# Two columns of x turned by VectorE from 32x32 blocks, and squares summed by ScalarE, in the front of a transformer block

## The chip, the cores and the metric

The kernel runs on one core of a Trainium2 chip. Its time is the device time of one execution in microseconds (us); the figure for a kernel is the median over its runs.

## What is computed

One layer of an encoder block in float32, with 1024 tokens and 1024 features. The part that the change touches is the first normalisation and the start of the combined projection:

```python
def rmsnorm(x, g):
    xf = x.astype(jnp.float32)
    y = xf * lax.rsqrt(jnp.mean(xf * xf, axis=-1, keepdims=True) + EPS)
    return (y * g.astype(jnp.float32)).astype(x.dtype)

h = rmsnorm(x, g_pre_mix[l])
proj = jnp.einsum('bsd,de->bse', h, w_in[l]) + b_in[l]
aq, ak, av, bq, bk, bv = jnp.split(proj, splits, axis=-1)
out_a = mixer_a(...)   # sliding window, 8 query heads on 2 key heads
out_b = mixer_b(...)   # chunked attention, 8 heads
y = jnp.einsum('bse,ed->bsd', mix, w_out[l])
x = x + rmsnorm(y, g_post_mix[l])
h = rmsnorm(x, g_pre_mlp[l])
u = jnp.square(jax.nn.relu(jnp.einsum('bsd,df->bsf', h, w_up[l])))
y = jnp.einsum('bsf,fd->bsd', u, w_down[l])
x = x + rmsnorm(y, g_post_mlp[l])
```

## The kernel before, in words

All engines run lists of instructions that are written out by hand and wait for each other by semaphores. SP's queue issues nearly all DMAs, in the order of its list; a wait in that list holds back every DMA behind it. TensorE (PE) multiplies, VectorE (DVE) and ScalarE (ACT) prepare its operands and take its results.

Every product is made of three, to keep float32 precision: an operand is split into a high part, rounded to the format `F32R`, and a low part, the difference. ScalarE makes the high parts (`x_hi`, `w1_hi`, `wv_hi`), VectorE the low ones (`x_lo`, `w1_lo`, `wv_lo`). The helper `three` issues the three matmuls; its lines in the trace are L2163, L2164 and L2165.

The front of the kernel goes by columns of x. A column k is 128 features of all 1024 tokens, 512 KB. It is loaded into `xraw[:, k]` with tokens on partitions, as eight tiles of 128 tokens. The matmul wants features on partitions, so TensorE turns each tile with a transpose (`x_transposes`, L2175, eight instructions for a column) into two PSUM banks. ScalarE copies the banks times the gain g to `x_hi` (L1064), VectorE forms `x_lo` (L1493), and TensorE then makes `first_products(k)`: three tiles of 128 outputs, two halves of 512 tokens, three matmuls each, 18 in all. TensorE's list per round is: transposes of column k + 1, products of column k. In the last round the transposes are those of `rcols` instead (L2235), a copy of 1/rms of each token spread over 128 columns, whose turning gives the row `rrow` by which the products are scaled later. After that come the value projections of two token tiles (48 matmuls of 320 columns each), which need `wv_hi` and `wv_lo` of all eight columns, and then attention.

The norm itself: ScalarE squares column k in one instruction of 1024 elements to one of two buffers (`square`, L1041), VectorE adds it to `sumsq` (`add_squares`, L1478). With all eight added, VectorE reduces over the 128 lanes of a tile (L1501) to `ss1`, one number for each token, ScalarE takes the root (L1069), VectorE forms 1/rms in five small steps (`rstd`, from L628) and writes the eight tiles of `rcols` (L1507). The tables `SQUARES` and `ADDED` say with which column each engine does what.

SP's queue loads the eight columns of x and the first weights in turn, then the tables, five of the value weights (`load_values`, 320 KB each), nine small constants and a bias row. It then waits until the last column is turned and squared, since the last three value weights are loaded over `xraw`. Behind them stand the stores and replication of the attention bias (`bias_rows`, `bias_a_rep`), the weights of a later tile (`load_fill(0)`, L698) and the biases of the first scores (`bias_a`, L681).

An exchange of 32x32 blocks followed by VectorE's transpose, which turns each 32x32 block by itself, is used further on in the kernel already: for attention probabilities (64 KB a DMA) and for the rows of the second norm (`hs`, 128 KB a DMA, L833, turned at L1790). There the data goes through a DRAM scratch and comes back in pieces of 32 floats.

## Time and profile before

| | before |
|---|---|
| median of three runs (lowest, highest) | 1037.47 us (1037.4, 1037.55) |
| the profiled execution: its time, its span | 1037.82 us, 1036.0 us |
| TensorE matmuls busy | 1026.4 us, 99% of the span |
| TensorE weight loads busy | 854.0 us, 82% |
| VectorE busy | 771.1 us, 74% |
| ScalarE busy | 467.8 us, 45% |
| GpSimd busy | 214.9 us, 21% |
| granted TensorE clock, mean | 0.998 of full |
| moved by DMA | 147.92 MB, 143 GB/s in the mean |

The span runs from the first to the last instruction that the profiler recorded; the time of the execution holds 1.8 us more. Busy time of TensorE overlaps itself, as matmuls are pipelined, so the distance from one start to the next is the cost of a matmul in a full list, not its length.

### The profile page before, as it was taken

The numbers are of one execution on the slowest core, as the hardware profiler recorded it, in microseconds if no ns is written. First come the engines' busy times: TensorE is split into PE (matmuls) and PEld (weight loads), VectorE is DVE, ScalarE is ACT, GpSimd is POOL, SyncE is SP. The second block draws the span as 40 slices with busy tenths as digits, with TensorE's granted clock in tenths as the row PEclk, the third lists the DMA queues.
The fourth block names the chain that finished last, engine by engine and source line by source line (L and its number), as shares of the span: only waits on it lengthen the run. The fifth ranks groups of instructions, "written<-read, shape, count | busy, mean of one in ns | idle before, by whom it ended". The sixth has DMA issues, their size and how long they took to land.

```text
span 1036.0 us, 15823 instructions
## 1 busy us (share of the span) xinstructions
PE 1026.4 (99%) x5555; PEld 854.0 (82%) x5555; DVE 771.1 (74%) x1505; ACT 467.8 (45%) x961; POOL 214.9 (21%) x200
## 2 busy tenths in 40 slices
PE   9999999999999999999999999999999999999997
PEld 7899887788777888888888888888888888888886
DVE  5855678766679478889988788786444777778997
ACT  5532255554478477846131121221344444444562
POOL 0400000000000003148676675672100000000000
PEclk9999999999999999999999999999999999999999
DMA  9454552110062365135444434436777733454344
GB/s 250 118 134 131 120 134 62 49 65 22 27 183 84 101 184 163 41 127 208 173 168 158 170 128 160 163 133 215 252 240 240 242 95 99 138 193 142 97 139 167
DMA packets 123894, 147.92 MB, mean 143 GB/s; under 512 B 56976, under 2 KB 74264, under 8 KB 121768
## 3 DMA queue, kind: packets, MB, share of 16 engines
q1 hardware_dynamic: 123128, 146.71, 44.8%
q8 instruction: 45, 0.74, 0.3%
q14 instruction: 33, 0.27, 0.1%
q10 hardware_dynamic: 688, 0.20, 0.1%
HBM read 103.65 MB, written 47.49 MB: 146 GB/s over the span
## 4 chain that ended last, share of the span: by engine, by line
PE 96%; issue 1%; DVE 1%; ACT 1%; DMA 0%; SPq 0%; DVEq 0%; ACTq 0%
PE ps L2163 28%; PE ps L2165 28%; PE ps L2164 28%; PE ps L2376 3%; PE ps L2362 2%; PE ps L2343 2%; PE ps L2287 1%; PE ps L2322 1%; PE ps L2495 1%; PE ps L2497 1%; PE ps L2483 1%; PE ps L2175 1%; DMA xraw<-in_x 0%; PE ps L2513 0%; PE ps L2300 0%
## 5 line engine op out<-in xcount | busy, mean ns | idle before, releaser
L2164 PE MATMUL ps<-tm_lo,sm_hi 128*128 128x512 f32 (+1 forms) x450 | 174.6, 388 | 0.0
L2165 PE MATMUL ps<-tm_hi,sm_lo 128*128 128x512 f32 (+1 forms) x450 | 174.6, 388 | 0.0
L2163 PE MATMUL ps<-tm_hi,sm_hi 128*128 128x512 f32 (+1 forms) x450 | 174.6, 388 | 0.0
L2163 PE MATMUL ps<-b_hi,wc_hi 128*128 128x512 f32 x448 | 174.6, 390 | 0.0
L2165 PE MATMUL ps<-b_hi,wc_lo 128*128 128x512 f32 x448 | 174.3, 389 | 0.0
L2164 PE MATMUL ps<-b_lo,wc_hi 128*128 128x512 f32 x448 | 174.3, 389 | 0.0
L1419 ACT ACTIVATE sm_hi<-sm_raw 128x512 fp32r<-128x512 f32 x112 | 70.7, 631 | 162.0 <-DMA sm_raw<-u_matrices 162.0
L2067 DVE TENSOR_TENSOR sm_lo<-sm_raw,sm_hi 128x512 fp32r<-128x512 f32 x112 | 77.7, 693 | 78.3 <-ACT sm_hi L1419 77.7
L2165 PEld LDWEIGHTS ps<-tm_hi,sm_lo 128*128 128x128 f32 x450 | 84.5, 188 | 17.5
L2163 PEld LDWEIGHTS ps<-tm_hi,sm_hi 128*128 128x128 f32 x450 | 84.5, 188 | 17.5
L2163 PEld LDWEIGHTS ps<-b_hi,wc_hi 128*128 128x128 f32 x448 | 84.1, 188 | 17.8 <-DVE wc_lo L1839 0.3
L2164 PEld LDWEIGHTS ps<-tm_lo,sm_hi 128*128 128x128 f32 x450 | 84.5, 188 | 17.3
L2164 PEld LDWEIGHTS ps<-b_lo,wc_hi 128*128 128x128 f32 x448 | 84.1, 188 | 17.5
L2165 PEld LDWEIGHTS ps<-b_hi,wc_lo 128*128 128x128 f32 x448 | 84.1, 188 | 17.3
L1331 ACT ACTIVATE p1s<-ps 128x512 f32<-128x512 f32 x16 | 9.6, 598 | 181.1 <-PE ps L2165 175.4
L2069 DVE TENSOR_TENSOR tm_lo<-w,tm_hi 128x512 fp32r<-128x512 f32 x112 | 76.7, 684 | 0.0
L1839 DVE TENSOR_TENSOR wc_lo<-up_raw,wc_hi 128x512 fp32r<-128x512 f32 x48 | 56.6, 1202 | 19.6 <-ACT wc_hi L1271 19.6
L1839 DVE TENSOR_TENSOR wc_lo<-wc_raw,wc_hi 128x512 fp32r<-128x512 f32 x64 | 68.9, 1080 | 2.5 <-POOL wc_raw L993 2.5
L1428 ACT ACTIVATE tm_hi<-w 128x512 fp32r<-128x512 f32 x112 | 69.0, 616 | 0.0
L985 POOL TENSOR_TENSOR wc_raw<-up_raw 128x512 f32<-128x512 f32 x16 | 22.4, 1402 | 221.1 <-DVE small L656 138.4
L2163 PE MATMUL ps<-x_hi,wf_hi 128*128 128x512 f32 x160 | 66.7, 417 | 0.0
L2165 PE MATMUL ps<-x_hi,wf_lo 128*128 128x512 f32 x160 | 62.7, 392 | 0.0
(239 smaller groups left out, 2062.4 us busy)
## 6 DMA issues: line engine op xcount, KB each, us to landing
u_matrices<-stage SPq DMA_DIRECT2D x112, 256.0 KB, 2.0
sm_raw<-u_matrices SPq DMA_DIRECT2D x112, 256.0 KB, 2.6
up_raw<-in_w_up SPq DMA_DIRECT2D x16, 1024.0 KB, 5.0
w<-in_w_down SPq DMA_DIRECT2D x64, 256.0 KB, 3.7
w_raw<-in_w_in SPq DMA_DIRECT2D x8, 512.0 KB, 3.4
xr<-in_x SPq DMA_DIRECT2D x8, 512.0 KB, 4.7
x_rows<-xr SPq DMA_DIRECT2D x8, 512.0 KB, 5.5
xf<-x_rows SPq DMA_DIRECT2D x8, 512.0 KB, 3.5
```

The costliest lines, as they stand in the source:

```text
L985: nc.gpsimd.tensor_tensor(wc_raw[s][5][:], a21, a22, ALU.add).then_inc(s_wsum, 1)
L1419: nc.scalar.activation(sm_hi[r][:], sm_raw[r][:], ACT.Copy).then_inc(s_shi, 1)
L1428: nc.scalar.activation(tm_hi[r][:], down_weights[q][c][:], ACT.Copy).then_inc(s_thi, 1)
L1839: nc.vector.tensor_tensor(wc_lo[s][p][:], src, wc_hi[s][p][:].bitcast(F32), ALU.subtract).then_inc(s_wlo[s], 1)
L2067: nc.vector.tensor_tensor(sm_lo[r][:], sm_raw[r][:], sm_hi[r][:].bitcast(F32), ALU.subtract).then_inc(s_slo, 1)
L2069: nc.vector.tensor_tensor(tm_lo[r][:], down_weights[q][c][:], tm_hi[r][:].bitcast(F32), ALU.subtract).then_inc(s_tlo, 1)
L2163: pe.matmul(out, w_hi_, x_hi_, start=start, stop=False)
L2164: pe.matmul(out, w_hi_, x_lo_, start=False, stop=False)
L2165: return pe.matmul(out, w_lo_, x_hi_, start=False, stop=stop)
L2343: last = pe.matmul(score_of(n, hh)[:, c * width:(c + 1) * width], q[rows, tok], k[rows, keys], start=(i == 0), stop=(i == 2))
L2362: last = pe.transpose(ps[:, bank, i * P:(i + 1) * P], prob_of(n, hh)[:, c0 + k * P:c0 + (k + 1) * P], ident[:])
L2376: last = pe.matmul(ps[64 * hh:64 * hh + 64, 7, (t % 4) * P:(t % 4) * P + P], v_tok[:, t + 1 - nk + k, at + 64 * hh:at + 64 * hh + 64], pro ...
```

## The change

Columns 6 and 7 of x are still loaded into `xraw` for their squares. In addition each is loaded straight from x by four DMAs (`load_x_blocks`) so that the 32x32 blocks lie exchanged in `x_blocks`, in pieces of 32 floats; VectorE's transpose of 128x1024 then gives `x_turned`, from which ScalarE and VectorE form `x_hi` and `x_lo` instead of from PSUM. TensorE's sixteen transposes of these columns are gone. The sum of squares is no longer formed by VectorE: ScalarE squares, for each tile of 128 tokens, four columns at a time (128x512) with a summed output, sixteen instructions, and VectorE adds the two halves. Two of the eight `rcols` tiles move from VectorE to ScalarE. The last three value weights are split in another place among the first tiles. The wait of SP ahead of their loads is now for column 5 turned and all sixteen squares.

```diff
--- before.py
+++ after.py
@@ -48,9 +48,7 @@
-SQUARES = ((0, 1), (2,), (3,), (4,), (5, 6), (7,), (), ())
-ADDED = ((), (1,), (2,), (3, 4), (5,), (6, 7), (), ())
+SQUARED = ((), (), (0, 1, 2, 3), (4, 5, 6, 7), (8, 9), (10, 11, 12), (13, 14, 15), ())
@@ -194,6 +192,13 @@
     return 4 + m % 2 if m < SINGLE else 4
+EXCHANGED = (6, 7)
+SPLIT_WITH = ((), (1,), (2,), (3,), (4,), (5, 6), (7,), ())
+VALUES_WITH = ((5,), (6, 7), (), (), (), ())
@@ -298,13 +303,14 @@
-        sumsq = sb("sumsq", 76, [P, T, P])
-        sq = sb("sq", 150.25, [P, 2, SEQ])
+        sq = sb("sq", 150.25, [P, 2, KH, P])
+        x_blocks = {k: sb(f"x_blocks{k}", at, [P, SEQ]) for k, at in zip(EXCHANGED, (76, 108))}
+        x_turned = {k: sb(f"x_turned{k}", at, [P, SEQ]) for k, at in zip(EXCHANGED, (112, 76))}
@@ -385,6 +391,12 @@
+        def blocks_landed(k):
+            return (s_xb, 64) if k == EXCHANGED[0] else (s_x0, 16 + 64)
+        def column(k):
+            return x_turned[k][:] if k in EXCHANGED else two(6)
         def load_first_weights(eng, g):
@@ -670,6 +682,12 @@
+            def load_x_blocks(k):
+                rows = x[:, k * P:(k + 1) * P].rearrange("(c j) (a i) -> a j c i", j=32, i=32)
+                for a in range(4):
+                    sp.dma_start(x_blocks[k][32 * a:32 * a + 32].rearrange("j (c i) -> j c i", i=32), rows[a]
+                                 ).then_inc(blocks_landed(k)[0], 16)
             def load_values(k):
@@ -688,7 +706,7 @@
                 if j == 0:
-                    sp.wait_ge(s_acc, KT - 1)
+                    sp.wait_ge(s_sq, 2 * T)
                 else:
@@ -726,7 +744,13 @@
             sp.dma_start(t5row[:], t5).then_inc(s_tab, 16)
-            for k in range(5):
+            load_values(0)
+            load_x_blocks(6)
+            load_values(1)
+            sp.wait_ge(s_xt, 2)
+            sp.wait_ge(s_sq, 1)
+            load_x_blocks(7)
+            for k in range(2, 5):
                 load_values(k)
@@ -737,8 +761,8 @@
             sp.dma_start(vrow.rearrange("a p -> p a"), b_in[:, AV:AV + 5], allow_slow_non_contiguous=True).then_inc(s_bv, 16)
-            sp.wait_ge(s_xt, column_done(KT - 1))
-            sp.wait_ge(s_sq, KT)
+            sp.wait_ge(s_xt, column_done(EXCHANGED[0] - 1))
+            sp.wait_ge(s_sq, 2 * T)
             for k in range(5, KT):
@@ -1032,14 +1056,17 @@
-            def square(k):
-                act.wait_ge(s_in[k], 16)
-                if k == 0:
+            def square_rows(n):
+                first, t = n // T * KH, n % T
+                if t == 0:
+                    for k in range(first, first + KH):
+                        act.wait_ge(s_in[k], 16)
                     act.wait_ge(s_x0, 16)
-                if k >= 3:
-                    act.wait_ge(s_acc, k - 2)
-                nc.scalar.activation((sq[:, k % 2] if k else sumsq[:].rearrange("p t n -> p (t n)")),
-                                     xraw[:, k].rearrange("p t n -> p (t n)"), ACT.Square).then_inc(s_sq, 1)
+                if n >= 2:
+                    act.wait_ge(s_sq, n - 1)
+                nc.scalar.activation(sq[:, n % 2], xraw[:, first:first + KH, t], ACT.Square,
+                                     accum_out=(ya1 if first else ss1)[:, t:t + 1]).then_inc(s_sq, 1)
@@ -1061,14 +1088,19 @@
                     act.wait_ge(s_xt, column_done(k))
-                    nc.scalar.activation(x_hi[:, k], two(6), ACT.Copy, scale=g1[:, k:k + 1]).then_inc(s_xhi, 1)
-                if k:
-                    first_hi(k)
+                    nc.scalar.activation(x_hi[:, k], column(k), ACT.Copy, scale=g1[:, k:k + 1]).then_inc(s_xhi, 1)
+                for j in SPLIT_WITH[k]:
+                    first_hi(j)
+                for n in SQUARED[k]:
+                    square_rows(n)
                 if k == KT - 2:
...
                     nc.scalar.activation(std1, ss1, ACT.Sqrt, bias=epsc, scale=1.0 / D).then_inc(s_std1, 1)
-                for n in SQUARES[k]:
-                    square(n)
+                if k == KT - 1:
+                    act.wait_ge(s_ch1, 1 + STEP)
+                    for t in range(T - 2, T):
+                        last = nc.scalar.activation(rcols[:, t * P:(t + 1) * P], ones[:], ACT.Copy, scale=rs1[:, t:t + 1])
+                    last.then_inc(s_rcol, 1)
                 if k >= 4:
@@ -1086,10 +1118,9 @@
             act.wait_ge(s_bsc, 1)
-            for k in range(5, KT):
-                value_hi(k)
-                tile_hi(k - 5)
-            for i in range(3, 2 * FIRST_TILES):
+            for i in range(2 * FIRST_TILES):
+                for k in VALUES_WITH[i]:
+                    value_hi(k)
                 tile_hi(i)
@@ -1470,13 +1501,6 @@
-            def add_squares(k):
-                dve.wait_ge(s_sq, k + 1)
-                if k >= 2:
-                    dve.wait_ge(s_acc, k - 1)
-                total = sumsq[:].rearrange("p t n -> p (t n)")
-                nc.vector.tensor_tensor(total, total, sq[:, k % 2], ALU.add).then_inc(s_acc, 1)
             dve.wait_ge(s_g1, 16)
@@ -1490,20 +1514,23 @@
                     dve.wait_ge(s_xhi, column_done(k))
-                    nc.vector.scalar_tensor_tensor(out=x_lo[:, k], in0=two(6), scalar=g1[:, k:k + 1],
+                    nc.vector.scalar_tensor_tensor(out=x_lo[:, k], in0=column(k), scalar=g1[:, k:k + 1],
                                                    in1=x_hi[:, k].bitcast(F32), op0=ALU.mult, op1=ALU.subtract
                                                    ).then_inc(s_xlo, 1)
-                    first_lo(k)
-                for n in ADDED[k]:
-                    add_squares(n)
+                    if k < EXCHANGED[0]:
+                        first_lo(k)
+                if k + 1 in EXCHANGED:
+                    dve.wait_ge(*blocks_landed(k + 1))
+                    nc.vector.transpose(x_turned[k + 1][:], x_blocks[k + 1][:]).then_inc(s_xt, 1)
+                    first_lo(k + 1)
                 if k == KT - 2:
-                    dve.wait_ge(s_acc, KT - 1)
-                    nc.vector.tensor_reduce(out=ss1, in_=sumsq[:], axis=mybir.AxisListType.X, op=ALU.add).then_inc(s_ss1, 1)
+                    dve.wait_ge(s_sq, 2 * T)
+                    nc.vector.tensor_tensor(ss1, ss1, ya1, ALU.add).then_inc(s_ss1, 1)
                     dve.wait_ge(s_std1, 1)
...
                     dve.wait_ge(s_id, 3)
-                    for t in range(T):
+                    for t in range(T - 2):
                         last = nc.vector.tensor_scalar(rcols[:, t * P:(t + 1) * P], ones[:], rs1[:, t:t + 1], None, ALU.mult)
@@ -1551,8 +1578,8 @@
             for i in range(2 * FIRST_TILES):
-                if i < 3:
-                    value_lo(5 + i)
+                for k in VALUES_WITH[i]:
+                    value_lo(k)
                 tile_lo(i)
@@ -2226,11 +2253,11 @@
             for k in range(1, KT):
-                if k + 1 < KT:
+                if k + 1 < EXCHANGED[0]:
                     x_transposes(k + 1)
-                else:
-                    pe.wait_ge(s_xlo, column_done(k))
-                    pe.wait_ge(s_rcol, 1)
+                elif k == KT - 1:
+                    pe.wait_ge(s_xlo, column_done(EXCHANGED[0] - 1))
+                    pe.wait_ge(s_rcol, 2)
                     for t in range(T):
```

On SP's queue, after the loads of x and the tables: what stood there before, the value loads of columns 0 to 4 (`wv_raw_111` to `wv_raw_115`) and the first small ones, is this.

```order
L674 DMA wv_raw_111<-in_w_in 128x5x128
L674 DMA wv_raw_112<-in_w_in 128x5x128
L674 DMA wv_raw_113<-in_w_in 128x5x128
L674 DMA wv_raw_114<-in_w_in 128x5x128
L674 DMA wv_raw_115<-in_w_in 128x5x128
L731 DMA small<-in_g_pre_mlp 128x8
L732 DMA small<-in_sinks 128x8
L734 DMA small<-in_b_in 64x2
L735 DMA small<-in_b_in 64x2
L734 DMA small<-in_b_in 64x2
L735 DMA small<-in_b_in 64x2
L736 DMA small<-in_b_in 128x2
```

In the changed kernel the same place reads as follows; `x_blocks_126` and `x_blocks_127` are the blocks of columns 6 and 7, and `wv_raw_110` is now the value load of column 0.

```order
L692 DMA wv_raw_110<-in_w_in 128x5x128
L688 DMA x_blocks_126<-in_x 32x32x32 x4
L692 DMA wv_raw_111<-in_w_in 128x5x128
L688 DMA x_blocks_127<-in_x 32x32x32 x4
L692 DMA wv_raw_112<-in_w_in 128x5x128
L692 DMA wv_raw_113<-in_w_in 128x5x128
L692 DMA wv_raw_114<-in_w_in 128x5x128
L755 DMA small<-in_g_pre_mlp 128x8
L756 DMA small<-in_sinks 128x8
L758 DMA small<-in_b_in 64x2
```

Eight DMAs now stand ahead of the value weights of columns 2 to 4 and of all that follows.

On VectorE, rounds 5 to 7 before, from the low part of column 5 to that of column 7 (the line of dots stands for four of the small steps of 1/rms):

```order
L1493 SCALAR_TENSOR_TENSOR x_lo<-ps,small,x_hi 128x1024
L1470 TENSOR_TENSOR w_lo<-w_raw,w_hi 128x384
L1478 TENSOR_TENSOR sumsq<-sumsq,sq 128x1024 x2
L1493 SCALAR_TENSOR_TENSOR x_lo<-ps,small,x_hi 128x1024
L1470 TENSOR_TENSOR w_lo<-w_raw,w_hi 128x384
L1501 TENSOR_REDUCE small<-sumsq 128x8
L628 TENSOR_SCALAR small<-small 128x8
...
L1507 TENSOR_SCALAR rcols<-ones,small 128x128 x8
L1493 SCALAR_TENSOR_TENSOR x_lo<-ps,small,x_hi 128x1024
```

And in the changed kernel, over the same rounds, with the same four steps left out:

```order
L1517 SCALAR_TENSOR_TENSOR x_lo<-ps,small,x_hi 128x1024
L1501 TENSOR_TENSOR w_lo<-w_raw,w_hi 128x384
L1524 STREAM_TRANSPOSE x_turned_128<-x_blocks_126 128x1024
L1501 TENSOR_TENSOR w_lo<-w_raw,w_hi 128x384
L1517 SCALAR_TENSOR_TENSOR x_lo<-x_turned_128,small,x_hi 128x1024
L1524 STREAM_TRANSPOSE x_turned_129<-x_blocks_127 128x1024
L1501 TENSOR_TENSOR w_lo<-w_raw,w_hi 128x384
L1528 TENSOR_TENSOR small<-small 128x8
L640 TENSOR_SCALAR small<-small 128x8
...
L1534 TENSOR_SCALAR rcols<-ones,small 128x128 x6
L1517 SCALAR_TENSOR_TENSOR x_lo<-x_turned_129,small,x_hi 128x1024
```

The additions and the reduction are gone; two transposes stand ahead of the low parts of columns 6 and 7, the second ahead of the small steps of 1/rms.

On ScalarE, rounds 5 to 7 before, from the high part of column 5 on:

```order
L1064 ACTIVATE x_hi<-ps,small 128x1024
L1050 ACTIVATE w_hi<-w_raw 128x384
L1041 ACTIVATE sq<-xraw 128x1024
L1046 ACTIVATE wv_hi_104<-wv_raw_112 128x640
L1064 ACTIVATE x_hi<-ps,small 128x1024
L1050 ACTIVATE w_hi<-w_raw 128x384
L1069 ACTIVATE small<-small 128x8
L1046 ACTIVATE wv_hi_105<-wv_raw_113 128x640
L1064 ACTIVATE x_hi<-ps,small 128x1024
L1050 ACTIVATE w_hi<-w_raw 128x384
L1046 ACTIVATE wv_hi_106<-wv_raw_114 128x640
```

And in the changed kernel:

```order
L1091 ACTIVATE x_hi<-ps,small 128x1024
L1077 ACTIVATE w_hi<-w_raw 128x384 x2
L1068 ACTIVATE sq,small<-xraw 128x512 x3
L1073 ACTIVATE wv_hi_103<-wv_raw_111 128x640
L1091 ACTIVATE x_hi<-x_turned_128,small 128x1024
L1077 ACTIVATE w_hi<-w_raw 128x384
L1068 ACTIVATE sq,small<-xraw 128x512 x3
L1098 ACTIVATE small<-small 128x8
L1073 ACTIVATE wv_hi_104<-wv_raw_112 128x640
L1091 ACTIVATE x_hi<-x_turned_129,small 128x1024
L1102 ACTIVATE rcols<-ones,small 128x128 x2
L1073 ACTIVATE wv_hi_105<-wv_raw_113 128x640
```

The squares of column 7 in round 5 have become three of the sixteen short ones, and three more stand in round 6 ahead of the root.

## Rows read from the trace of the kernel before

**Rows 1.** The page, part 4: the chain that ended last, by engine.

```profile
PE 96%; issue 1%; DVE 1%; ACT 1%; DMA 0%; SPq 0%; DVEq 0%; ACTq 0%
```

**Rows 2.** Timeline of TensorE: start us, length us, engine, line, what.

```profile
37.31 1.03 PE L2175 MATMUL ps<-ident,xraw 128*128 128x128 f32 x8
...
42.06 0.40 PE L2165 MATMUL ps<-x_hi,w_lo 128*128 128x512 f32 x1
42.29 1.04 PE L2235 MATMUL ps<-ident,rcols 128*128 128x128 f32 x8
...
43.40 0.39 PE L2164 MATMUL ps<-x_lo,w_hi 128*128 128x512 f32 x1
...
47.29 0.30 PE L2163 MATMUL ps<-wv_hi,x_hi 128*128 128x320 f32 x1
```

**Rows 3.** Timeline of VectorE in the same stage, idle time before in brackets.

```profile
29.56 1.28 DVE L1493 SCALAR_TENSOR_TENSOR x_lo<-ps,small,x_hi 128x1024 fp32r<-128x1024 f32 x1 [2.11 <-ACT x_hi L1064]
30.76 0.55 DVE L1470 TENSOR_TENSOR w_lo<-w_raw,w_hi 128x384 fp32r<-128x384 f32 x1
31.22 2.55 DVE L1478 TENSOR_TENSOR sumsq<-sumsq,sq 128x1024 f32<-128x1024 f32 x2
...
37.78 0.17 DVE L628 TENSOR_SCALAR small<-small 128x8 f32<-128x8 f32 x1 [0.37 <-ACT small L1069]
...
38.71 1.66 DVE L1507 TENSOR_SCALAR rcols<-ones,small 128x128 f32<-128x128 f32 x8
40.28 1.28 DVE L1493 SCALAR_TENSOR_TENSOR x_lo<-ps,small,x_hi 128x1024 fp32r<-128x1024 f32 x1
```

**Rows 4.** Timeline of ScalarE in the same stage.

```profile
28.41 1.11 ACT L1064 ACTIVATE x_hi<-ps,small 128x1024 fp32r<-128x1024 f32 x1 [0.95 <-PE ps L2175]
29.42 0.51 ACT L1050 ACTIVATE w_hi<-w_raw 128x384 fp32r<-128x384 f32 x1
29.84 1.05 ACT L1041 ACTIVATE sq<-xraw 128x1024 f32<-128x1024 f32 x1
30.78 0.72 ACT L1046 ACTIVATE wv_hi<-wv_raw 128x640 fp32r<-128x640 f32 x1
```

**Rows 5.** Timeline of ScalarE near the end, a square with a summed output.

```profile
1002.08 0.61 ACT L1400 ACTIVATE dump<-y 128x512 f32<-128x512 f32 x1
...
1002.69 0.62 ACT L1419 ACTIVATE sm_hi<-sm_raw 128x512 fp32r<-128x512 f32 x1
```

**Rows 6.** Timeline of SP's queue.

```profile
32.01 0.64 SPq L739 DMA_DIRECT2D value_bias_row<-in_b_in  x1
38.38 1.52 SPq L674 DMA_DIRECT2D wv_raw<-in_w_in  x3
...
57.52 5.72 SPq L681 DMA_DIRECT2D bias_a<-bias_a_rep  x8
```

**Rows 7.** Stretches: us, engines busy, granted clock, DMA share, GB/s.

```profile
24.00:28.00 4.00, 4.00 (x23) 3.33 (x22) 2.89 (x3) 3.45 (x5) 2.72 (x6) 1.00 1.19 290
28.00:32.00 4.00, 4.00 (x21) 3.36 (x20) 2.44 (x3) 3.10 (x4) 4.00 (x18) 1.00 0.47 93
...
355.00:356.00 1.00, 1.00 (x6) 0.84 (x5) 0.90 (x6) 0.00 (x0) 0.00 (x0) 1.00 0.78 122
...
367.00:368.00 1.00, 1.00 (x6) 0.84 (x5) 0.99 (x1) 0.98 (x1) 0.00 (x0) 1.00 1.07 168
```

**Rows 8.** The tile hs: durations min/median/max in ns, times to landing in us.

```profile
L833 SPq DMA_DIRECT2D hs<-h_row_tiles x16: 562/683/1490, 353.5 to 389.6; - x16
...
L1790 DVE STREAM_TRANSPOSE ps<-hs x4: 1259/1260/1262, 359.3 to 392.5; 128x1024 f32<-128x1024 f32 x4
...
DMA to landing us min/median/max: 2.6/2.9/4.8
```

**Rows 9.** Timelines of ScalarE and of VectorE, value stage and first scores.

```profile
45.09 0.74 ACT L1046 ACTIVATE wv_hi<-wv_raw 128x640 fp32r<-128x640 f32 x1 [0.69 <-DVE small L1514]
...
66.79 0.55 DVE L1547 SCALAR_TENSOR_TENSOR v_tok<-ps,small,bv 128x320 f32<-128x320 f32 x1 [3.02 <-PE ps L2165]
```

More of the change, by code:

```diff
@@ L498, in build @@
         s_sc = sem("sink_columns_ready")
-        s_x0 = sem("first_column_second_half_landed")
+        s_x0 = sem("first_column_second_half_then_last_blocks_landed")
         s_in = [sem(f"x_columns_then_wo_landed{n}") for n in range(KT)]
@@ L502, in build @@
         s_xt = sem("x_columns_transposed")
+        s_xb = sem("x_blocks_landed")
         s_xhi = sem("x_hi_ready")
@@ L508, in build @@
         s_sq = sem("squares_ready")
-        s_acc = sem("squares_added")
-        s_ss1 = sem("sumsq_reduced")
+        s_ss1 = sem("sumsq_halves_added")
         s_std1 = sem("std1_ready")
```

## The prediction

> **What bounds the kernel now.** I read the page first: TensorE is on 96% of the chain that ended last, and DMA, VectorE and ScalarE hold a per cent or less each [rows 1]. So only what shortens TensorE's own list of work, or makes it wait, can move the time. Then TensorE's timeline in the stage that the diff touches. There it never pauses: matmuls of 512 columns start every 0.229 us ((47.29 - 43.40) / 17), and the eight transposes of one column sit between two of them. From 42.06, the last matmul of a round, to 43.40, the second of the next, is 1.34 us; two plain steps would be 0.46, so eight transposes cost 0.88 us [rows 2]. The one of 37.31 us is the last that the diff removes (column 7), the one at 42.29 (the 1/rms columns) stays. Last I read the helpers, VectorE [rows 3] and ScalarE [rows 4], and SP's queue with the DMA engines' load [rows 6, 7], since they must now deliver columns 6 and 7 earlier than TensorE used to ask for them.
>
> **What is removed from TensorE.** Sixteen transposes, 2 x 0.88 = 1.76 us, on the path. Their inputs were waited for nowhere, so the whole of it is bare. Nothing is added on TensorE.
>
> **New deadlines.** Products of column 6 start at 37.31 - 0.88 = 36.4 us; a round takes 18 x 0.229 = 4.1, so the 1/rms columns are wanted at 42.29 - 1.76 = 40.5 and column 7 at 41.4.
>
> **VectorE.** It loses seven additions of squares (two take 2.55 us [rows 3]) and their reduction, and gains two transposes of 128x1024. The same shape runs later in the kernel at 1.26 us, into PSUM [rows 8]; I take 1.2 as step. Its new list: low part of column 5 from 29.56 (step 1.20), weights 0.46, done 31.2. Transpose 6 to 32.4 if its blocks have landed, weights 0.46; then ScalarE's high part of column 6 (step 1.01, 28.41 to 29.42 [rows 4]) from about 32.6 to 33.7, VectorE's low part 1.3 more: ready at 35.1, wanted at 36.4, so 1.3 us of slack. Put from the other end: blocks 6 may land as late as 32.5. Transpose 7 runs 35.1 to 36.3, weights to 36.8, then one small addition in place of the reduction, 0.4 for the root on ScalarE, 0.93 for the chain of small steps (37.78 to 38.71) and six columns at 0.2 (eight took 38.71 to 40.28 [rows 3]): 39.5, against 40.5. The low part of column 7 follows at once and ends at 40.7, against 41.4. Slack is 0.7 to 1.0 us. Blocks 7 may therefore land as late as 35.8 before TensorE waits at all.
>
> **ScalarE.** It loses eight squares of 1024 columns and gains sixteen of 512 with a summed output. The nearest rows are the same operation near the end of the kernel: from one such square to the next instruction is 0.61 us, its accumulator read included (1002.08 to 1002.69 [rows 5]). Sixteen are 9.8 us against 7.5 for eight at 0.94 (29.84 to 30.78 [rows 4]). From below the cost is nothing (the engine idles 0.95 us before the row at 28.41 [rows 4]); from above 2.3 us, if all of it stood in line. I take nothing, because each batch ends before ScalarE's next duty: in round 5 column 5 ends at 29.4, two weight splits of 0.42 (29.42 to 29.84) at 30.3, three squares at 32.1, one value split at about 32.8, and column 6 can't be asked for before 32.5. In round 6 the last three squares end at 36.1, before VectorE comes to their sum at 36.8. Two 1/rms columns go to ScalarE after its high part of column 7 (37.9 to 38.9): about 39.4, inside the 40.5. If this cover were gone, each 0.61 us of lateness in round 6 would eat the 1.0 us of slack first.
>
> **The block loads.** Four DMAs of 128 KB in pieces of 128 bytes per column. The trace has the same shape once more, the second exchange of rows in 32x32 blocks: 0.56 to 1.49 us to issue each, median 0.68, and 2.6 to 4.8 us to land [rows 8]. While such loads had the DMA engines for themselves they moved 168 GB/s with the engines fully busy, or 122 GB/s in a window where they were not [rows 7]. So 512 KB takes 3.1 to 4.3 us of the engines. At 24 to 28 us these are saturated at 290 GB/s, and a little after 29 us the load falls away (93 GB/s over 28 to 32 [rows 7]); the first value weights go before the blocks, and I work out that their data is through at about 25 us (four more loads of 320 KB at 290 GB/s take 4.4 us, and all end at about 29.3). Then blocks 6 end at 28.1 to 29.3, one value load at 1.1 us, blocks 7 at 32.3 to 34.7, and 1 to 1.5 us to be seen: blocks 6 at 29 to 31 (limit 32.5), blocks 7 at 33.3 to 36.2 (limit 35.8). I take the lower end, since 168 is the rate at full load and full load is what stands here: no wait. The upper end costs 0.4 us. VectorE waits for the blocks in its own list: behind each wait stand that column's transpose, a weight split and its low part, behind the second also the whole 1/rms chain, and TensorE waits for both. SP's new wait ahead of blocks 7, for column 0 turned and the first square (a matter of round 2), is over long before SP gets there.
>
> The Trainium skill (DMA: Bandwidth & Descriptors, Specifications) says that a piece needs at least 512 bytes to run at line rate, below which the engine reads, modifies and writes. By that rule these loads are dear for their size; the trace agrees in kind, 168 GB/s beside 290. The page gives no price for 128 bytes, so by it alone the sum would stay 1.76 us or lose a stall that it does not size.
>
> **SP's queue.** The eight issues add 2 x 2.7 (median) to 2 x 6.0 us ahead of value weights 2 to 4, the constants, the last value weights and the bias rows. SP used to reach the last value loads at 32.65 and sat 5.7 us until the transpose of column 7 (38.38 [rows 6]). The new condition (all squares, 36.1) is earlier, so the queue passes there at 38.1 to 44.6; I take about 39.5, nearer the median [rows 8]. That is 1 us later than before, 3 us against an earlier TensorE. Who waits: the value split of column 5 ran at 45.09 [rows 9], and TensorE comes to its products after 30 matmuls of 320 columns, an estimate of 30 x 0.229 x 320/512 = 4.3 us behind 47.29 - 1.76, so at 49.8; then the bias of the first scores, issued at 57.52. Behind those scores VectorE idles 3.02 us before 66.79 [rows 9], which takes in the 3 us. Cost nothing; at the upper end (6.2 us late) the value splits of columns 5 to 7 would come about 2 us late, which just eats the gain.
>
> **Sum.** The profiled execution took 1037.82 us, 1036.0 of span and 1.8 around it; less 1.76 that is a span of 1034.2 and 1036.1 in all. It lies 0.35 above the median of the runs, so on the median: 1037.47 - 1.76 = 1035.7 us. 0.2% is 2.1 us, about what a measurement of this kernel can tell from no change: the likeliest case lies just inside it.
>
> **Rivals.**
> *Part of the gain turns into a wait for blocks.* TensorE stands before column 6 or 7 because blocks 7, or SP's late value weights, pass the limits above. For it: the upper end of the load (36.2 against 35.8), slacks of only 0.7 to 1.3 us, three engines in the loop. Against: every median leaves room. Price 0.3 to 1.7 us: 1036.0 to 1037.4. Here also the case that the removed transposes were free, 1037.5, which the unbroken row of starts [rows 2] all but excludes. Chance 0.14.
> *The small pieces are much dearer from x than from the scratch.* The rows of x are 4 KB apart and the engines are already full. If a column took 7 us instead of 3.1 (75 GB/s), blocks 6 would be seen at 33, blocks 7 at 41.5: 5.7 us past the limit, and the total is 1037.47 - 1.76 + 5.7 = 1041.4. It decides at 1.76 us past the limit, blocks 7 at 37.6, which is about 5 us a column. For it: the skill's rule above leans this way, without a size. Against: 122 GB/s is the worst that the rows show. Chance 0.09, of which 0.07 lies over 0.2%.
> *More than the transposes comes back.* TensorE idles 9.6 us of the span in all (1036.0 - 1026.4 busy), mostly at both ends, and about 1 us of that is short waits for the attention stage's helpers. They may fall otherwise after the shift. 0.4 to 1.1 us more: 1034.6 to 1035.3. Nothing in the diff aims there. Chance 0.13.
> *Forecast*, all slack holds: 0.64, with its own range of 1035.4 to 1036.0.
>
> **Numbers.** Leaving out the dearest-pieces case and the far ends, the range is 1034.8 (part of the third rival) to 1037.2 (most of the first). Faster by over 0.2% (below 1035.4): 0.13 from the third rival and 0.05 from the forecast's edge, 0.18. Slower by over 0.2%: 0.07. Within: 0.75.
>
> **What the profile after would show.** Products of column 6 start at 36.4 and the value products at 45.5 instead of 47.29, with no idle ahead of them: right. VectorE's transpose 6 starts at 31.2 directly behind the weights; if instead it idles for a DMA, the block price is wrong. Squares 0.61 us apart with no gap. SP passes the last value loads at 38 to 41; if far later, the queue is the cause. TensorE idle ahead of a matmul of column 6 or 7, or of a value product, proves a rival; a span that shrinks by 1.76 in the first 50 us but not at the end shows a wait given back later.

## The result, and the profile after

The change made the kernel slower. Its median is 1044.12 us (1042.66 to 1046.93, 6 runs) beside 1037.51 us (1037.4 to 1038.44, 6 runs) of the kernel before: a ratio of 1.0065, 95% interval 1.0055 to 1.0076, where 1035.7 us was forecast and 1037.2 was the upper end of the range. The profiled execution took 1044.56 us with a span of 1042.8, against 1037.82 and 1036.0. In the kernel after, most line numbers of TensorE's part are 27 higher.

In the chain that ended last TensorE had 96% [rows 1]. Part 4 of the page now shows

```profile
PE 87%; SPq 4%; DVE 3%; issue 3%; DMA 2%; ACT 1%; DVEq 0%; ACTq 0%
```

TensorE's longest waits between 30 and 400 us, with the total, how many there were, and the longest. Neither existed before:

```profile
PE ps L2190 <- DVE wv_lo L1496: 4.2, 2, 4.0
PE ps L2349 <- DVE probT_a L1622: 0.4, 1, 0.4
```

Its timeline shows where the 4 us stand, and what comes after them:

```profile
40.36 0.85 PE L2262 MATMUL ps<-ident,rcols 128*128 128x128 f32 x6
...
49.89 0.31 PE L2192 MATMUL ps<-wv_hi,x_lo 128*128 128x320 f32 x1
54.18 0.64 PE L2190 MATMUL ps<-wv_hi,x_hi 128*128 128x320 f32 x1 [3.98 <-DVE wv_lo L1496]
54.62 0.47 PE L2191 MATMUL ps<-wv_lo,x_hi 128*128 128x320 f32 x1
54.88 0.47 PE L2192 MATMUL ps<-wv_hi,x_lo 128*128 128x320 f32 x1
...
59.66 0.31 PE L2190 MATMUL ps<-wv_hi,x_hi 128*128 128x320 f32 x1
59.81 0.31 PE L2191 MATMUL ps<-wv_lo,x_hi 128*128 128x320 f32 x1
...
66.78 0.33 PE L2314 MATMUL ps<-ak_hi,aq_hi 64*128 64x128 f32 x2
```

The reader is to see three things. At 40.36, where the 1/rms columns are turned, TensorE is 1.93 us earlier than before (42.29 [rows 2]): so far the change does what it says. At the products of the sixth value column it stands still until 54.18. And the matmuls behind the wait start 0.27 us apart until 59.66 and 0.15 apart from there on. The windows give the cause of the last: the granted clock is 0.50 of full speed, the lower level of 1.2 GHz, after the engine had done nothing for four microseconds (columns as in [rows 7]).

```profile
50.00:52.00 2.00, 0.20 (x2) 0.00 (x0) 0.00 (x0) 0.00 (x0) 0.00 (x0) 1.00 0.74 136
52.00:54.00 2.00, 0.00 (x0) 0.00 (x0) 0.70 (x1) 1.35 (x2) 0.00 (x0) 0.68 0.87 226
54.00:56.00 2.00, 1.82 (x6) 1.57 (x6) 1.90 (x4) 0.74 (x1) 0.00 (x0) 0.50 0.64 215
56.00:58.00 2.00, 1.78 (x7) 1.63 (x7) 1.36 (x3) 1.81 (x3) 0.00 (x0) 0.50 0.17 53
58.00:60.00 2.00, 2.00 (x11) 2.00 (x10) 1.79 (x3) 0.87 (x2) 0.00 (x0) 0.62 0.51 167
60.00:62.00 2.00, 2.00 (x16) 2.00 (x14) 1.47 (x3) 0.72 (x1) 0.00 (x0) 1.00 0.69 229
```

Who is late? The wait names VectorE's `wv_lo`, VectorE waits for ScalarE's `wv_hi`, and ScalarE's row leads on to a DMA:

```profile
52.53 0.74 ACT L1073 ACTIVATE wv_hi<-wv_raw 128x640 fp32r<-128x640 f32 x1 [10.04 <-DMA wv_raw<-in_w_in]
```

SP's queue issued that load in good time, at 40.88, inside the 38 to 41 that the prediction gave as right:

```profile
28.23 4.57 SPq L688 DMA_DIRECT2D x_blocks<-in_x  x4
...
40.14 0.64 SPq L763 DMA_DIRECT2D value_bias_row<-in_b_in  x1
40.88 1.71 SPq L692 DMA_DIRECT2D wv_raw<-in_w_in  x3
42.64 2.21 SPq L769 DMA_DIRECT2D bias_rows<-arow  x1
44.90 0.28 SPq L770 DMA_DIRECT2D bias_rows<-brow  x1
50.31 0.35 SPq L772 DMA_DIRECT2D bv<-value_bias_row  x1
55.80 0.77 SPq L774 DMA_DIRECT2D bias_a_rep<-bias_rows  x1
```

The row that matters is the one ahead of it. `value_bias_row` copies 640 numbers from `b_in` to a DRAM scratch, 2.5 KB, each number a piece of 4 bytes. The tile's view gives its time from issue to landing as the largest of two (the other is `bv`), first after, then before:

```profile
DMA to landing us min/median/max: 6.6/8.4/10.2
```
```profile
DMA to landing us min/median/max: 4.9/7.1/9.4
```

Between its issue and its landing at 50.3 hardly anything else arrives. The same windows view of after, then of before while the row runs alone, in the last stretch that it holds and just behind it:

```profile
41.00:50.00 9.00, 8.99 (x52) 7.96 (x50) 5.40 (x10) 1.49 (x2) 0.19 (x1) 1.00 0.39 22
```
```profile
32.00:38.00 6.00, 6.00 (x36) 5.07 (x35) 4.76 (x7) 2.08 (x4) 5.57 (x11) 1.00 0.09 1
39.00:41.00 2.00, 2.00 (x11) 1.65 (x10) 2.00 (x8) 2.00 (x4) 0.00 (x0) 1.00 0.01 2
41.00:44.00 3.00, 3.00 (x19) 2.58 (x18) 3.00 (x5) 0.81 (x2) 0.00 (x0) 1.00 0.82 230
```

Before, the slow row was issued at 32.01, and 6.4 of its 9.4 us were over when SP, having waited 5.7 us for something else, issued the value loads at 38.38 [rows 6]; their data came from 41 on, at 230 GB/s. What was left of the row cost nothing there: when ScalarE split the first of these weights at 45.09, it had waited for VectorE and not for the load [rows 9]. The sign was there to be read: 2 GB/s over 39 to 41, with three loads of 320 KB issued. After, the eight block issues fill SP's idle stretch, the row goes out 8.1 us later (32.01 to 40.14), directly ahead of the same loads, and for nine microseconds the core moves 22 GB/s.

### The profile page after: what moved, and what is told of

It reads as the page before. It is cut to its first block, busy times and chain, and to the rows that moved or that the text cites. A ratio compares the mean times of both kernels' runs of the same rounds, so it can differ in the third digit from the quotient of the medians.

```text
span 1042.8 us, 15810 instructions
## 1 busy us (share of the span) xinstructions
PE 1028.9 (99%) x5539; PEld 854.5 (82%) x5539; DVE 763.9 (73%) x1498; ACT 470.6 (45%) x987; POOL 213.0 (20%) x200
## 4 chain that ended last, share of the span: by engine, by line
PE 87%; SPq 4%; DVE 3%; issue 3%; DMA 2%; ACT 1%; DVEq 0%; ACTq 0%
PE ps L2190 26%; PE ps L2192 25%; PE ps L2191 25%; PE ps L2403 2%; PE ps L2389 2%; PE ps L2370 2%; DMA wv_raw<-in_w_in 1%; SPq L688 1%; SPq L679 1%; PE ps L2522 1%; PE ps L2524 1%; PE ps L2510 1%; PE ps L2314 1%; SPq L410 1%; ACT score_a L1144 1%
## 5 line engine op out<-in xcount | busy, mean ns | idle before, releaser
L2191 PEld LDWEIGHTS ps<-tm_lo,sm_hi 128*128 128x128 f32 x450 | 84.5, 188 | 17.5
L2190 PEld LDWEIGHTS ps<-tm_hi,sm_hi 128*128 128x128 f32 x450 | 84.5, 188 | 17.4
L2192 PEld LDWEIGHTS ps<-tm_hi,sm_lo 128*128 128x128 f32 x450 | 84.5, 188 | 17.2
```

The costliest lines, as they stand in the source:

```text
L2190: pe.matmul(out, w_hi_, x_hi_, start=start, stop=False)
L2191: pe.matmul(out, w_hi_, x_lo_, start=False, stop=False)
L2192: return pe.matmul(out, w_lo_, x_hi_, start=False, stop=stop)
```

## The experiments

The theory after this reading: the whole loss comes from the place of the slow row, and its half clock and later waits follow from that. The rivals: that the value loads are late for another reason (blocks of 128 bytes, full queues), that the squares on ScalarE hold something back, and that the gain itself is not there. Each ratio below is to the kernel before as measured beside that run. Its median was 1037.18 us beside the first four, 1037.48 beside the next four and 1037.38 beside the last four, so a difference of two times from different groups is good to some 0.3 us.

**The row taken out of SP's queue.** The changed kernel, with the row issued by ScalarE's queue near the start:

```diff
-            sp.dma_start(vrow.rearrange("a p -> p a"), b_in[:, AV:AV + 5], ...).then_inc(s_bv, 16)
             load_first_weights(act, 0)
+            act.dma_start(vrow.rearrange("a p -> p a"), b_in[:, AV:AV + 5], ...).then_inc(s_bv, 16)
```

> The changed kernel, with one DMA moved: the store of the value bias row (2.5 KB, 640 elements of 4 bytes, 10.2 us from issue to landing) is issued by ScalarE's queue behind the first weights instead of by SP's queue just ahead of the last three value loads. Theory (slow row): these loads move nothing until the row has landed; with the row gone from their way the value products don't wait, TensorE starts the first scores near 59.8 us instead of 66.8, and the time is about 1035.7 us. Rival (block loads): the eight block loads make SP's queue and the DMA engines late by themselves; the time stays above 1041. Second possibility inside the theory: the row slows the first loads of x wherever it is issued; then TensorE starts late by up to 10 us and the time is above 1040, with idle before 10 us.

Measured 1042.55 us, ratio 1.0052 (1.0035 to 1.0068). The wait at the value products is gone, but a new one stands at the front:

```profile
PE ps L2202 <- DMA xraw<-in_x: 5.1, 1, 5.1
```

So the row's cost moved with it, which is the second of the cases that I had put down. It lands after 11.0 us here, and the loads of x, on SP's queue, are late.

**The kernel before, with only the row moved.** It goes from its old place to directly ahead of the last three value loads, behind SP's wait:

```diff
-            sp.dma_start(vrow.rearrange("a p -> p a"), b_in[:, AV:AV + 5], ...).then_inc(s_bv, 16)
             sp.wait_ge(s_xt, column_done(KT - 1))
             sp.wait_ge(s_sq, KT)
+            sp.dma_start(vrow.rearrange("a p -> p a"), b_in[:, AV:AV + 5], ...).then_inc(s_bv, 16)
```

> The kernel before, with no block loads and no other squares; only the store of the value bias row is issued after SP's wait for the last column (at about 38.4 us) instead of ahead of it (32.0). Theory (slow row): the row lands at 48.5, the value weights of column 5 at about 50.6 instead of 44, ScalarE splits them near 50.7; TensorE wants them at 51.7 with a low part 1.5 us after the split, so it waits 0.5 to 3 us over columns 5 to 7 and, through the clock that falls in such a wait, may lose 1 us more: 1038 to 1041. Rival (block loads): nothing in the kernel before is late, 1037.5.

Measured 1043.37 us, ratio 1.0059 (1.0044 to 1.0074), with no block and no square changed:

```profile
PE ps L2163 <- DVE wv_lo L1465: 2.3, 3, 1.5
```

One moved line makes a slowdown of the size of the whole change's. That is more than the 1038 to 1041 that I had expected: the wait was in the range, the clock was not. The granted clock over 50 to 60 is 0.74. After pauses of 0.33 and 1.62 us, neither as long as the changed kernel's, the matmuls from 54.87 on start 0.27 apart until 61.48. These 21 steps take 6.61 us, against 3.09 at full clock; 0.85 of the difference is the third pause and 2.7 the low clock, where I had put 1.

**The changed kernel with a fast row.** The same bytes in 128 pieces of 20 bytes, in the order in which they are read. The value biases land in another order; that part of the computation is changed.

```diff
-            sp.dma_start(vrow.rearrange("a p -> p a"), b_in[:, AV:AV + 5], ...).then_inc(s_bv, 16)
+            sp.dma_start(bass.AP(vrow.tensor, 0, [[5, P], [1, 5]]), b_in[:, AV:AV + 5]).then_inc(s_bv, 16)
```

> The changed kernel, with the bias row stored at its place in SP's queue in 128 pieces of 20 bytes instead of 640 of 4 bytes, so that the row's values stand in another order: the output leaves out the right order of the value biases, all else is computed. Theory (slow row): it is the number of tiny elements that takes the 10 us; with a fifth of them it lands in 2 to 4 us, the value loads at 43 to 45, and the time is about 1035.7 to 1036.5. If 20-byte pieces are as slow as the 4-byte ones in total, the time stays near 1044. Rival (block loads): above 1041.

Measured 1036.63 us, ratio 0.9994 (0.9984 to 1.0003): 7.5 us below the changed kernel, though not clearly below the one before, and 0.1 above my range. The row lands after 3.0 us, and over 43 to 50 us the core moves 193 GB/s. The first scores start at 59.34, 2.1 us earlier than before (61.46). But the lead does not last: TensorE's products of probabilities and values of one round start at 97.4, 2.1 us earlier than before, and its first transposes of probabilities at 145.3, only 0.6 earlier. Between the two stands

```profile
120.82 0.44 PE L2349 MATMUL ps<-probT_a,v_odd 128*64 128x128 f32 x4 [0.65 <-DVE probT_a L1622]
```

**The control: the kernel before, row issued by ScalarE's queue.** The edit is that of the first experiment, on the kernel before.

> The kernel before, with only the store of the value bias row issued by ScalarE's queue at the start. A control for the first run: theory (slow row) says that in the kernel before the row drained while SP waited for the last transposes, so moving it changes nothing: 1037.5 within 0.5. If the row at the start disturbs the first loads of x, this kernel shows it without anything else: slower by as much.

Measured 1044.11 us, ratio 1.0064 (1.0049 to 1.0079). I had expected no change, and missed: a DMA on ScalarE's queue delayed loads on SP's. The same stretch, first with the row in it, then in the kernel before without it:

```profile
6.00:16.00 10.00, 6.05 (x25) 4.81 (x26) 3.07 (x5) 5.00 (x8) 0.00 (x0) 0.80 1.14 137
```
```profile
6.00:16.00 10.00, 9.19 (x51) 7.73 (x52) 6.40 (x9) 8.14 (x11) 0.00 (x0) 1.00 1.09 263
```

The DMA engines are as busy in both and move half as much. So it is not the order of one queue that holds the loads back. The Trainium skill (DMA: Bandwidth & Descriptors, Issuing engines are not separate DMA queues) says that DMAs of all issuers run on the same engines; this run agrees, 137 beside 263 GB/s.

**What makes the row slow.** Two more shapes of it in the changed kernel. Five transfers of one row each:

```diff
+            for n in range(5):
+                sp.dma_start(vrow[n:n + 1].rearrange("a p -> p a"), b_in[:, AV + n:AV + n + 1], ...).then_inc(s_bv, 16)
```

> The changed kernel, the value biases' row written by five transfers of one row of 128 elements each, all still of 4 bytes and issued at the same place. Theory A (each 4-byte element costs about 16 ns whatever transfer it is in, and the loads behind wait for all of them): the five together end after about 10 us, five issues of 0.6 us push the value loads some 2.5 us later still on SP's queue, PE's wait at the fifth value product stays 4 us or grows to 6: 1044 to 1046. Theory B (one transfer of this form goes through one DMA engine's ring, five are spread over several engines): each ends in about 2 us, all within 4 us, PE's wait at the value products falls to 0 to 1.5 us: 1037 to 1039.

Measured 1045.33 us, ratio 1.0074 (1.006 to 1.0088); the wait is 5.8 us, and the slowest of the five lands after 10.6. Theory A, as expected. And the list of elements turned, so that the writes are contiguous:

```diff
+            sp.dma_start(vrow, b_in[:, AV:AV + 5].rearrange("p a -> a p"), ...).then_inc(s_bv, 16)
```

> The changed kernel, the value biases' row listed in the order of its target (five rows of 128, contiguous where it is written, 4-byte pieces 72 bytes apart where it is read), the same bytes at the same place. Theory A (the count of 4-byte elements sets the time, on whichever side they are scattered): landing still 9 to 11 us, 1043.5 to 1045, no change. Theory B (the scattered 4-byte writes alone are slow, since the reads were never contiguous for more than 20 bytes): landing 3 to 5 us, PE's wait below 1 us, 1036.5 to 1038.

Measured 1049.17 us, ratio 1.0107 (1.0094 to 1.0121), worse than either theory gave. SP, which waits for the row before it loads `bv`, passes there at 54.08, 14.8 us after the row's issue at 39.24. So scattered writes are not the point, since with contiguous ones the row was slower; but the mere count of elements does not set the time either, since it is 640 in both. What sets it beyond "pieces of 4 bytes" was not tried. The Trainium skill (DMA: Bandwidth & Descriptors, Why a DMA increments its semaphore by 16 and not by 1) has a rule that would fit: the number of engines is taken from the slowest dimension of the pattern, which is 128 in the one and 5 in the other. No run here shows on how many engines a transfer ran.

**The price of the half clock.** TensorE is kept busy in its wait, with 18 more matmuls whose result nobody reads:

```diff
+                    if t == 0 and k == 5:
+                        pe.wait_ge(s_et, 2)
+                        for _ in range(18):
+                            pe.matmul(ps[:, 4, :], x_hi[:, 0, 0:P], x_hi[:, 0, 0:512], start=True, stop=True)
```

> The changed kernel, with 18 more matmuls of 512 columns by TensorE into a bank that nobody reads, just ahead of the products of value column 5, in the 4 us in which it waits there. Theory A (the loss has two parts: the wait itself, and about 1 us because the matmuls from 54.2 to 59.5 run at half clock after it, 0.267 against 0.147 us each): the added matmuls take about 4 us, the wait shrinks to under 0.5 us, the steps behind it are 0.147 us, and the time is 1042.6 to 1043.4, about 1 us less than the changed kernel. Theory B (the clock falls for other reasons, or PE catches up later anyhow): 1043.8 to 1044.8, no less.

Measured 1043.12 us, ratio 1.0052 (1.0039 to 1.0065). The clock stays up behind the wait:

```profile
54.00:56.00 2.00, 0.98 (x6) 0.71 (x6) 1.90 (x4) 1.84 (x3) 0.00 (x0) 1.00 0.22 74
56.00:58.00 2.00, 1.97 (x13) 1.97 (x14) 1.90 (x3) 0.71 (x2) 0.00 (x0) 1.00 0.50 178
```

Thirteen matmuls in two microseconds where there were seven, and the first product of probabilities starts at 84.5 instead of 86.3. The profiled executions differ by 1.8 us, the medians by 1.0, and their intervals overlap. Of the 1.8 us, 0.3 are there already at the first product behind the wait (53.84 for 54.18), where the clock has not yet made a difference. So that the clock stays up is shown, what it is worth only roughly. Part of what it gains goes to a second wait of 1.05 us, for the next value column.

**The squares alone.** ScalarE's sixteen squares, with both columns turned by TensorE as before and no block loads (`EXCHANGED = ()`, and the conditions that go with it):

> The second half of the change alone: the squares summed by ScalarE per token tile, columns 6 and 7 of x turned by TensorE as before, the loads as before. SP's queue has no block loads, so the row is issued at about 32.0 and ends in SP's wait as before. Theory A (the order of the row and the value loads is the whole loss; squares and sums are hidden): 1036.9 to 1037.6, PE waits for nothing at the value products. Theory B (the squares on ScalarE, 16 pieces of 0.6 us, hold back x_hi and with it PE, and this is part of the loss): over 1038, with waits of PE for x_hi or for the columns of 1/rms.

Measured 1037.74 us, ratio 1.0002 (0.9993 to 1.0011), no wait at the value products, the row back at 31.55. That is 0.1 above the range of theory A and below that of theory B, and its interval runs from -0.7 to +1.1 us: within it the squares cost and gain nothing.

**A fast row with the output whole, in both kernels.** The row is stored as it is read and replicated in that order, and GpSimd, idle at that time, puts it into the values' order with one copy:

```diff
+            sp.dma_start(vrow, b_in[:, AV:AV + 5]).then_inc(s_bv, 16)
...
+            pool.wait_ge(s_bv, 32)
+            nc.gpsimd.tensor_copy(bv[:].rearrange("p (a n) -> p a n", n=P), bv_raw[:].rearrange("p (n a) -> p a n", a=5)
+                                  ).then_inc(s_bv, 1)
```

> The kernel before, with the value biases' row stored as it is read (128 pieces of 20 bytes), replicated in that order, and put in the values' order by one copy of 640 elements on GpSimd, so that the output is whole. Theory A (in the kernel before the row's 9.4 us lay under SP's wait, so a short row is worth nothing there): 1037.2 to 1037.7, no difference. Theory B (the row cost the kernel before something too, and part of what the changed kernel gains without it has nothing to do with the change): 1036.4 to 1037.0, below the kernel before by 0.5 or more.

> The changed kernel with the same row in 20-byte pieces and the copy on GpSimd, output whole. Theory A (the whole loss is the slow row; what is left of the change gains 2.1 us at the first scores and keeps about 0.5 at the end): 1036.4 to 1037.0, PE waits for nothing at the value products, the first values on VectorE not later for GpSimd's copy. Theory B (the row's order left out in the earlier run hid a cost: the copy, some 1 to 2 us on GpSimd between the row's landing and the first values, and the masks of the biases behind it): 1037.5 to 1039.

Before: 1037.55 us, ratio 1.0001 (0.9992 to 1.001). After: 1037.24 us, ratio 0.9997 (0.9989 to 1.0006). A fast row is worth nothing to the kernel before, where the slow one lay under a wait, and 6.9 us to the changed one (1044.12 - 1037.24). The second figure is 0.2 above what I expected. GpSimd's copy ran from 48.92 for 2.03 us, ahead of its use. That the row held the loads back in the kernel before too can now be seen over 39 to 41, where 2 GB/s flowed with the slow row. With the fast one it is 277, in the kernel before:

```profile
39.00:41.00 2.00, 2.00 (x11) 1.65 (x10) 2.00 (x7) 1.69 (x4) 0.00 (x0) 1.00 0.92 277
```

These two runs are also the fairer pair for the lead, since they differ in the change alone and the profiled execution of the kernel before ran some 0.6 us late from the front on (1/rms columns at 42.3 where this pair's kernel before has 41.7). The lead is 1.5 us at the first scores (59.3 against 60.8), still 1.5 at 97.4, 0.1 at 145.2, and 0.3 in the span (1035.4 against 1035.7).

**Where the lead went.** The wait of the fast-row kernel for `probT_a` leads on VectorE to `wf_lo` just ahead of it, and from there to ScalarE and a load (timelines of the changed kernel with GpSimd's copy):

```profile
113.08 1.35 SPq L717 DMA_DIRECT2D w_raw<-in_w_in  x2
117.61 1.06 ACT L1181 ACTIVATE wf_hi<-w_raw 128x1024 fp32r<-128x1024 f32 x1 [7.30 <-DMA w_raw<-in_w_in]
118.71 1.23 DVE L1705 TENSOR_TENSOR wf_lo<-w_raw,wf_hi 128x1024 fp32r<-128x1024 f32 x1 [6.70 <-ACT wf_hi L1181]
119.85 0.70 DVE L1627 STREAM_TRANSPOSE probT_a<-prob_a 128x512 f32<-128x512 f32 x1
```

In the kernel before the load is issued at 113.03 and the transpose starts at 119.83: this chain does not come earlier when TensorE does. In the kernel before with the same fast row it is even 0.8 to 0.9 us earlier (112.16 and 119.06), though TensorE is later there. The lead is lost one round ahead, where SP stores probabilities and waits for them to land before it reloads them. First the changed kernel, then the kernel before, both with the fast row:

```profile
95.19 0.33 SPq L731 DMA_DIRECT2D prob_round_tiles<-prob_a  x1
100.78 2.65 SPq L735 DMA_DIRECT2D prob_a<-prob_round_tiles  x4
```
```profile
96.23 0.33 SPq L713 DMA_DIRECT2D prob_round_tiles<-prob_a  x1
100.76 2.67 SPq L717 DMA_DIRECT2D prob_a<-prob_round_tiles  x4
```

The store is issued 1.04 us earlier and takes 5.6 us to land where it took 4.5, so the reload starts at the same time. Why this store is slower is open.

In the next round SP waits for the exchange of probabilities in the same way, and issues the load of `w_raw` behind it. So the load is put into that wait:

```diff
                 sp.dma_start(p_dram[m], first_probs(r)...).then_inc(s_hst, 16)
+                if between is not None:
+                    load_fill(between)
                 sp.wait_ge(s_hst, 48 + 16 * (m + 1))
...
-            exchange_probs(4)
-            load_fill(1)
+            exchange_probs(4, 1)
```

> The run above, and the load of w_raw for fill 1 issued on SP between the store and the reload of round 4's probabilities instead of behind the reload. Theory A (the 2.1 us are given back because w_raw, issued at 113.3 wherever PE stands, holds wf_hi, wf_lo and the turning of the probabilities behind them): w_raw issued at about 108.3 to 110, wf_hi 3 to 5 us earlier, PE does not wait for probT_a at 120.8, and the time is 1.0 to 1.5 below the run above: 1035.0 to 1035.7. Theory B (the pace there is set by the exchange of the probabilities itself, its store and reload one after the other on SP's queue): 1036.4 to 1037.2, no less than the run above, with PE's wait for probT_a still there or moved to a later round.

> The kernel before with the short row and with the earlier load of fill 1: the two helps without the change. Theory A (they only matter where TensorE comes 2 us earlier; before, it waits for nothing there): 1037.1 to 1037.7. Theory B (the earlier fill gains by itself): 1036.0 to 1036.8.

The changed kernel with both: 1035.88 us, ratio 0.9987 (0.9978 to 0.9996). The kernel before with both: 1037.31 us, ratio 0.9999 (0.999 to 1.0008). The same rows of the first:

```profile
108.90 1.32 SPq L717 DMA_DIRECT2D w_raw<-in_w_in  x2
...
116.81 0.70 DVE L1628 STREAM_TRANSPOSE probT_a<-prob_a 128x512 f32<-128x512 f32 x1
```

TensorE waits for nothing between 100 and 150, and its lead holds. Against the kernel before with both helps it is 0.8 us at the first scores (59.8 against 60.6), 0.8 at 144.2, 0.6 at 393.5 and 0.8 in the span (1034.5 against 1035.3). The medians of the two lie 1.4 apart. This is the one version here that beats both kernels, by 1.5 us in the medians (the interval of its ratio is 0.4 to 2.3 us) and by 8.2; it is 0.2 above the range that I had put down.

## Why the prediction was wrong

**The step that failed** is "SP's queue", with its words "Cost nothing". It counted the block issues right in kind (9.5 us in all, inside the 5.4 to 12), put the last value loads at "about 39.5" (40.88) and drew the bound from that: at most 6.2 us late, about 2 us of wait. But it went by issue times alone. It named the constants and the bias row as moved, and never asked how long the row takes to land, nor what it lies beside in its new place. The row's issue at 32.01 and SP's wait behind it were both on the table [rows 6], and the tile's own view would have given 9.4 us. The issues did not delay the loads much; they took away the cover of a transfer behind which the large loads hardly move: 10.2 us from issue to landing, a wait of 4.1 us in TensorE's list, and the low clock behind it. The Trainium skill (DMA: Bandwidth & Descriptors, Rules for kernel authors) warns that a last dimension that is not contiguous becomes one descriptor for each element. The trace agrees, 10.2 us beside 3.0 in pieces of 20 bytes, and I did not weigh it, because the diff does not touch that line.

**The size.** From the run with pieces (first scores at 59.34) to the changed kernel (66.78) are 7.4 us. From the last matmul before the wait to the next start, 49.89 to 54.18, are 4.29 us where a step is 0.15, so 4.14. The 18 starts from 54.18 to 59.66 take 5.48 us, against 18 x 0.147 = 2.64 at full clock: 2.84 more, of which a second short wait is 0.4 and the low clock 2.4. Together 7.0; the rest, 0.5, stood before the wait (value products from 45.64 for 45.17). A wait in TensorE's list was priced in the prediction at its own length; here the clock added more than half of it again.

**The rivals.** The first named the right place in half a sentence ("SP's late value weights") and priced it at 0.3 to 1.7 us, where it cost 7.4. The second, dear blocks, has about the right total (1041.4) for the wrong reason: the blocks landed in 3.8 to 5.0 us, and VectorE turned both without waiting for them. (The 2.6 to 4.8 us of [rows 8] are those of all DMAs of the tile `hs`, its stores too; the loads alone have 2.6 to 3.5, so these blocks were a little dearer than that shape.) VectorE's rows:

```profile
31.08 1.25 DVE L1524 STREAM_TRANSPOSE x_turned<-x_blocks 128x1024 f32<-128x1024 f32 x1
...
35.86 1.25 DVE L1524 STREAM_TRANSPOSE x_turned<-x_blocks 128x1024 f32<-128x1024 f32 x1
```

They stand at 31.1 for 31.2 and at 35.9 for 35.1. The third rival, more coming back, turned out the other way.

**What held.** "What is removed from TensorE" held: 1.76 was forecast, and the 1/rms columns came 1.93 us earlier, at 40.36 for 40.5. The size of this is better read over all runs whose front is undisturbed. In five kernels with TensorE's transposes (before, row late, squares alone, and the two with the fast row) the columns start at 41.5 to 42.3, in seven with the blocks at 39.8 to 40.4, and the means are 1.7 apart. VectorE's list held with less room than forecast: the low part of column 7 ended at 41.4, where 40.7 was forecast and 41.4 was the limit. ScalarE's squares, 34.93, 35.55, 36.16, are 0.61 apart and hidden; alone they are worth 0.0 (interval -0.7 to +1.1 us).

**What was left out besides.** Even with the slow row gone the whole of the 1.76 did not arrive, since 1.4 of a lead of 1.5 us are given back before 145 us (1.5 of 2.1 against the slower profile of before). The sentence "a span that shrinks by 1.76 in the first 50 us but not at the end shows a wait given back later" described it, but no chance stood beside it. The changed kernel shows it too: 5.4 us behind the kernel before at 104.9, and 6.5 at 152.4. The place where it is given back is the exchange of probabilities: a store that lands after 5.6 us for 4.5, and in the next round a reload that takes 3.3 us to issue for 2.6. No run tells why either is slower.

## What to carry to other kernels

When an edit adds DMAs to a queue, look at each DMA that it pushes back: not when it is issued but how long it takes to land, what hides that now, and which loads stand behind it in the new place. A copy whose pieces are single numbers is a hazard wherever it stands; store it as it is read, and let an idle engine reorder it on the chip. A lead won early is worth only what the next chain with its own clock lets through, so look along the trace for engines that already end just in time.

## What the runs showed of the hardware

- A DRAM-to-DRAM copy of 640 numbers in 4-byte pieces takes 9.4 to 11.4 us to land at each of the places in the two queues where it was issued, and 10.6 as five transfers; in 128 pieces of 20 bytes 2.0 to 3.0. In the order of its target it took 14.8.
- While it runs, large loads crawl, those on another queue too: 22 GB/s over 41 to 50 us and 2 GB/s over 39 to 41 where 277 flowed with the fast row, both on one queue; 137 GB/s with DMA engines at full share where 263 flowed without it, on two.
- After 4.1 us without work TensorE ran at 1.2 GHz for 5.5 us, though work was there all that time but for 0.4 us. After pauses of 0.33 and 1.62 us within three microseconds it ran at 1.2 GHz for 6.6 us. With matmuls in most of the wait the clock stayed at 2.4 GHz.
